# The first token half and two weight tiles of the second input projection, made ready inside the feed-forward's block

## The reference, cut to what matters

```
# end of the first block
h = rmsnorm(x, norm2_g)
u = h @ w_ffn_up
a, b = u[..., :D_FF], u[..., D_FF:]
a = causal_dwconv(a, ffn_conv_w, ffn_conv_b)
x = x + (silu(a) * b) @ w_ffn_down            # x2 in the kernel
x = rmsnorm(x, norm_f_g)                      # the first block's own last norm
# start of the second block
u = rmsnorm_2(x, norm1_g_2)
proj = u @ w_in_2                             # D_MODEL -> 37 tiles of 128 columns
x_r, y_r, c_q, c_kv, k_pe, g_a, g_b = split(proj)
x_r = causal_depthwise_conv(x_r, ...); h_r = rg_lru(x_r, ...)
```

## Time and profile before

| | us |
|---|---|
| median of 3 runs | 3498.38 |
| lowest and highest run | 3498.35, 3500.34 |
| the profiled execution, its time | 3503.13 |
| the profiled execution, its span | 3501.2 |
| TensorE busy in the span | 3125.2 (89%) |
| VectorE, ScalarE, GpSimd busy | 1609.1, 937.9, 440.9 |

### The profile page before, as it was taken

One profiled execution on the slowest core, in us unless ns is written; L12 is line 12 of the kernel. 1 busy time (PEld: TensorE's weight loads), 2 busy tenths in 40 slices (PEclk: granted clock), 3 DMA queues, 4 the chain that ended last, 5 costly groups with the idle time before them and its releaser, 6 DMA issues. The chain is left out here.

```text
span 3501.2 us, 47146 instructions
## 1 busy us (share of the span) xinstructions
PE 3125.2 (89%) x19758; PEld 2317.3 (66%) x19758; DVE 1609.1 (46%) x2278; ACT 937.9 (27%) x1349; POOL 440.9 (13%) x440
## 2 busy tenths in 40 slices
PE   7999779987999999997999997689979987878886
PEld 5778568876788888886778776466658863323232
DVE  6657335454566346634544445466543443111113
ACT  4333222223233222223333322133332211000000
POOL 2211002121000000002000001433201001111110
PEclk9999669998999999999999998799989997998997
DMA  3332331215333433334222234411046548999998
GB/s 124 115 127 97 122 93 29 74 33 183 108 97 98 140 123 97 97 118 141 79 82 75 79 114 154 165 61 61 31 144 208 181 151 320 423 423 424 424 391 342
DMA packets 147701, 555.41 MB, mean 159 GB/s; under 512 B 20544, under 2 KB 52992, under 8 KB 128424
## 3 DMA queue, kind: packets, MB, share of 16 engines
q1 hardware_dynamic: 105568, 426.79, 33.4%
q0 software_dynamic: 36800, 114.37, 8.7%
q10 hardware_dynamic: 5128, 11.30, 0.9%
HBM read 467.28 MB, written 105.02 MB: 163 GB/s over the span
## 5 line engine op out<-in xcount | busy, mean ns | idle before, releaser
L53 PE MATMUL in_acc<-in_x_hi,in_w_hi 128*128 128x512 f32 x1024 | 412.7, 403 | 40.4 <-DVE in_x_lo L1487 36.4
L55 PE MATMUL in_acc<-in_x_hi,in_w_lo 128*128 128x512 f32 x1024 | 403.3, 394 | 0.0
L54 PE MATMUL in_acc<-in_x_lo,in_w_hi 128*128 128x512 f32 x1024 | 403.3, 394 | 0.0
L1652 ACT CAST ff_w_hi<-ff_w_raw 128x1024 fp32r<-128x1024 f32 (+1 forms) x144 | 148.0, 1028 | 494.1 <-PE ff_acc L55 474.4
L53 PE MATMUL ff_acc<-ff_x_hi,ff_w_hi 128*128 128x512 f32 x704 | 275.3, 391 | 2.0 <-DVE ff_w_lo L1776 2.0
L54 PE MATMUL ff_acc<-ff_x_lo,ff_w_hi 128*128 128x512 f32 x704 | 274.6, 390 | 0.0
L55 PE MATMUL ff_acc<-ff_x_hi,ff_w_lo 128*128 128x512 f32 x704 | 274.4, 390 | 0.0
L53 PEld LDWEIGHTS in_acc<-in_x_hi,in_w_hi 128*128 128x128 f32 x1024 | 195.0, 190 | 92.3 <-issue 37.6
L1776 DVE TENSOR_TENSOR ff_w_lo<-ff_w_raw,ff_w_hi 128x1024 fp32r<-128x1024 f32 (+1 forms) x144 | 171.8, 1193 | 164.7 <-ACT ff_w_hi L1652 163.2
L54 PEld LDWEIGHTS in_acc<-in_x_lo,in_w_hi 128*128 128x128 f32 x1024 | 195.0, 190 | 44.7 <-issue 4.8
L55 PEld LDWEIGHTS in_acc<-in_x_hi,in_w_lo 128*128 128x128 f32 x1024 | 194.9, 190 | 41.4
(11 more groups left out here) (609 smaller groups left out, 5829.5 us busy)
## 6 DMA issues: line engine op xcount, KB each, us to landing
wide_b_lo<-in_w SPq DMA_DIRECT2D x24, 2048.0 KB, 40.0
wide_a_lo<-in_ew SPq DMA_DIRECT2D x48, 1024.0 KB, 37.8
wide_a_hi<-in_w SPq DMA_DIRECT2D x24, 2048.0 KB, 35.5
ff_w_raw<-in_w_up SPq DMA_DIRECT2D x88, 512.0 KB, 3.5
wide_b_hi<-in_w SPq DMA_DIRECT2D x20, 2048.0 KB, 36.7
in_w_raw<-in_w_in SPq DMA_DIRECT2D x64, 512.0 KB, 3.6
wide_w<-in_ew SPq DMA_DIRECT2D x20, 1024.0 KB, 38.5
ff_w_raw<-in_w_down SPq DMA_DIRECT2D x32, 512.0 KB, 3.6
```

Of the source, the lines that this page charges most:

```text
L53: pe.matmul(out, w_hi, x_hi, start=first, stop=False)
L54: pe.matmul(out, w_hi, x_lo, start=False, stop=False)
L55: return pe.matmul(out, w_lo, x_hi, start=False, stop=last)
L1652: nc.scalar.copy(w_hi[:, j % 3, 0:width], w_raw[:, j % 2, 0:width]).then_inc(w_hi_done, 1)
```

## The change

The second projection's preparations for the first 512 tokens move into the second half's down tiles of `feed_stage`, and what both stages use lies in tensors named `have_...` that outlive the feed-forward's block: `x_hi` and `x_lo` of 512 tokens, `w_raw`, `w_hi`, `w_lo`, both sums, the product of the gains and the squared inner gain.

In `feed_stage`, per down tile n of the second half: SyncE also loads the first half of tile n of x2; ScalarE makes `x_hi` and a square of it, and a square of the half tile that VectorE has just evicted (tile n - 1); VectorE makes `x_lo` and adds both squares into both sums. The units of weights are longer by two, the first two tiles of the second projection. GpSimd has nothing new.

In `in2` TensorE begins with the column matmuls, then makes the first two weight tiles over the first token half, spreads the factors, and then makes the same two tiles over the second token half. That half (`late_hi`, `late_lo`, from `late_raw`) is loaded and split in `in2` itself, behind the roots on ScalarE and behind the diagonals on VectorE. GpSimd's additions are gone.

```diff
-            load(0)
-            load(1)
-            for k in range(KT):
-                ...
-                sp.dma_start(x_raw[:, k % 4, :], src[k]).then_inc(x_loaded[k % 4], 16)
...
+                for k in range(KT):
+                    sp.dma_start(late_raw[:, k, :], src[k][:, HALF:]).then_inc(x_loaded[k], 16)
 # ScalarE of in2
+                for k in range(KT):
+                    act.wait_ge(x_loaded[k], 16)
+                    nc.scalar.activation(late_hi[:, k, :], late_raw[:, k, :], ACT.Copy, scale=gains[:, k:k + 1]).then_inc(x_hi_done, 1)
+                high_part(2)
             act.wait_ge(spread_ready, 1)
 # TensorE of in2
+                columns(0, sq_sum)
+                columns(DT, sum_2).then_inc(ss_ready, 1)
+                for k in range(KT):
+                    for j in range(2):
+                        mm = products(j, 0, k)
...
             mm.then_inc(spread_ready, 1)
+            if inner is not None:
+                for k in range(KT):
+                    pe.wait_ge(x_split, k + 1)
+                    for j in range(2):
+                        mm = products(j, 1, k)
...
             pe.wait_ge(rstd_ready, 2 if inner is not None else 1)
 # VectorE of in2
-                    dve.wait_ge(acc_ready, 2 * i + h + 1)
+                    dve.wait_ge(acc_ready, 2 * h + i + 1 if inner is not None and i < 2 else 2 * i + h + 1)
 # GpSimd of in2
-            for k in range(1, KT):
+            for k in range(1, KT if inner is None else 1):
 # feed_stage, weights
+    units += [(w, SEQ) for w in next_w]
 # SyncE of feed_stage
+            for k in range(DT):
+                sp.wait_ge(x_split, 2 * DT + k - 1)
+                if k >= 2:
+                    sp.wait_ge(half_sq_ready[0], k - 1)
+                sp.dma_start(x_raw[:, k % 2, :], x2[k][:, 0:HALF]).then_inc(x_loaded[k % 2], 16)
+                ...
+                        load(j)
 # ScalarE of feed_stage
+            def square_evicted(n):
+                act.wait_ge(acc_free, first_job["down", 1] + n + 1)
+                ...
+                nc.scalar.activation(half_sq[:, 1, n % 2, :], o_buf[:, n % 2, 0:HALF], ACT.Square).then_inc(half_sq_ready[1], 1)
...
+                    nc.scalar.activation(x_hi[:, n, :], x_raw[:, n % 2, :], ACT.Copy, scale=g).then_inc(x_hi_done, 1)
+                    if f == 1:
+                        ...
+                        nc.scalar.activation(half_sq[:, 0, n % 2, :], x_raw[:, n % 2, :], ACT.Square).then_inc(half_sq_ready[0], 1)
                     for c in range(CHUNKS):
                         high_part(j0 + CHUNKS * n + c + 3)
+                        if f == 1 and c == 0 and n >= 1:
+                            square_evicted(n - 1)
+            square_evicted(DT - 1)
 # VectorE of feed_stage
+            def add_half(h, n):
+                hs = slice(h * HALF, (h + 1) * HALF)
+                dve.wait_ge(half_sq_ready[h], n + 1)
+                ...
+                tt(sums[:, hs], sums[:, hs], half_sq[:, h, n % 2, :], ALU.add).then_inc(half_sum_ready[h], 1)
+                dve.wait_ge(half_sum_2_ready[h], n)
+                stt(out=sums_2[:, hs], in0=half_sq[:, h, n % 2, :], scalar=gain_sq[:, n:n + 1], in1=sums_2[:, hs], op0=ALU.mult,
+                    op1=ALU.add).then_inc(half_sum_2_ready[h], 1)
...
+                    if f == 1:
+                        add_half(0, n)
                     low_part(j0 + CHUNKS * n + 4)
+                    if f == 1 and n >= 1:
+                        add_half(1, n - 1)
...
+                    if f == 1 and n >= 2:
+                        dve.wait_ge(half_sq_ready[1], n - 1)
                     tt(o_buf[:, u, 0:HALF], acc[:, (q0 + n) % 4, :], aux[:, u, 0:HALF], ALU.add).then_inc(acc_free, 1)
+            add_half(1, DT - 1)
```

More of the change, by code:

```diff
@@ L1349, in norm_dense_stage @@
         aux = ctx.enter_context(nc.psum_tensor(f"{name}_aux", [P, 4, HALF], F32))
-        x_loaded = [sem(f"x_loaded{i}") for i in range(4)]
+        x_loaded = [sem(f"x_loaded{i}") for i in range(4 if inner is None else KT)]
         w_loaded = [sem(f"w_loaded{i}") for i in range(2)]
@@ new lines, in _ @@
+            if inner is None:
+                pe.wait_ge(w_lo_done, 2)
+                for k in range(KT):
+                    if k == KT - 1:
+                        pe.wait_ge(sum_ready, KT - 1)
+                        columns(0, sq_sum).then_inc(ss_ready, 1)
+                    pe.wait_ge(x_split, k + 1)
+                    for j in range(2):
+                        for h in range(NH):
+                            mm = products(j, h, k)
+                            if k == KT - 1:
+                                mm.then_inc(acc_ready, 1)
+            else:
+                columns(0, sq_sum)
+                columns(DT, sum_2).then_inc(ss_ready, 1)
+                for k in range(KT):
+                    for j in range(2):
+                        mm = products(j, 0, k)
@@ L1461, in _ @@
                 if i >= 2:
[L1462 removed]
+                    pe.wait_ge(w_lo_done, i + 1 - READY)
                     for h in range(NH):
@@ L1517, in _ @@
                                     ALU.mult).then_inc(diag_ready, 1)
+            if inner is not None:
+                for k in range(KT):
+                    dve.wait_ge(x_hi_done, k + 1)
+                    nc.vector.scalar_tensor_tensor(out=late_lo[:, k, :], in0=late_raw[:, k, :], scalar=gains[:, k:k + 1], in1=late_hi[:, k, :],
+                                                   op0=ALU.mult, op1=ALU.subtract).then_inc(x_split, 1)
+                low_part(2)
             side.vector_first(dve)
@@ L1639, in _ @@
                     load(j)
-            for j in range(first_unit["up", 1] + 3, NU):
+            for j in range(first_unit["up", 1] + 3, first_unit["down", 1] + 3):
                 load(j)
+            for u in range(2):
+                sp.wait_ge(stored[u], 16 * DT // 2)
+            for k in range(DT):
[3 more added lines that the diff above has]
+                sp.dma_start(x_raw[:, k % 2, :], x2[k][:, 0:HALF]).then_inc(x_loaded[k % 2], 16)
+                for c in range(CHUNKS):
+                    j = first_unit["down", 1] + 3 + CHUNKS * k + c
+                    if j < NU:
+                        load(j)
         @block.scalar
```

182 lines of the change are left out of this document (93 added, 89 removed).

## The result

Changed kernel: median 3488.12 us of 20 runs; kernel before, beside it: 3499.48 us of 20. The ratio is 0.9967, 95% interval 0.9959 to 0.9975: 0.33% or 11.4 us less, where 21.9 were forecast. The kernel is faster, as the likeliest sign was, but 3488.1 lies outside the range that ended at 3482.0.

A forecast was written before the change was run, and what follows sets the result against it. TensorE was taken to bound the second projection from tile i = 2 on; starting that tile 20.2 us earlier, plus 1.65 us of half clock, gave 21.9 us: 3498.4 less 21.9 is 3476.5 us, range 3470.5 to 3482.

The forecast's parts named there:

- The feed-forward's block at no cost: Feed-forward's down tiles: the added VectorE, ScalarE and load work fits into idle time, so the block ends as before.
- (a): From the feed-forward's last matmul (1620.8) to the second projection's first column matmul (1625.5): 4.7 us, as now.
- B: Rival, less gained: the feed-forward's block ends late (store's issue held) or half clock lasts longer; 3479 to 3481 us, chance 0.17.
- (b): Second projection's 32 one-column matmuls, 5 at full clock and 27 at half: 6.3 us.
- (c): Second projection's 48 matmuls over the first token half, 4.4 us of them at half clock: 13.0 us.
- (d): Second projection's two spreads of the factors, between the matmuls of both token halves: 3.5 us.
- (e): Second projection's 48 matmuls over the second token half, at 0.227 us each: 10.9 us.
- Behind i = 2 the half clock: Second projection, behind the start of tile i = 2: the half clock goes, as no wait stands ahead; 1.65 us gained.
- The gate's slack: Recurrent layer's gate behind tile i = 2: work of 10.0 us ahead of it against the tile's 10.9 leaves 0.9 us.
- A: Rival, faster: the second projection's column matmuls keep the clock up, 4.9 us less, 3471.6 us; chance 0.15.
- C: Rival, hardly a change: convolution's chain sets the pace, recurrent work gives time back; some 3492 to 3500 us, chance 0.04.
- D: Rival, slower: added VectorE work makes TensorE wait in each of the 8 down tiles; 3505 us, chance 0.03.

The follow-up runs named there:

- a_pad192: The changed kernel with 192 unused bytes per partition behind the shared tensors, and nothing else: 3478.6 us, ratio 0.9942.
- gains_first: The changed kernel with the two 32-byte tensors (gains, gain_sq) allocated ahead of the shared operands instead of behind them: 3481.8 us, ratio 0.9949.
- a_pad192_b: A repetition of a_pad192 with the same code: 3480.2 us, ratio 0.9942.
- warm_cols: a_pad192 with five unused 128x512 float32 matmuls behind the feed-forward's last product, in TensorE's idle time ahead of the columns: ratio 0.9932.
- a_pad32: The changed kernel with 32 unused bytes behind the shared tensors: 3495.8 us, ratio 0.9986.

## Why the prediction was right or wrong

**What bounds the kernel: right.** The seam and the projection stood on TensorE, and an earlier i = 2 was passed on.

**The feed-forward's block at no cost: right for the work, wrong for the block.** With the distance at zero and the added work in place, the feed-forward takes 814.5 us from its first to its last matmul in `a_pad192`, 814.9 in `gains_first` and 815.4 in `a_pad192_b`, against 814.4 before; the four kernels with other columns or unused matmuls have 812.6 to 815.2. So five operations on VectorE, three on ScalarE and the loads of each down tile cost nothing that could be told from the scatter of 1 us. But the changed kernel took 818.6: 3.2 us from the pace and about 1 from a longer half clock at the start. The sign "the last eviction of the feed-forward at the same time as now, to 0.5 us" failed: 1624.47 against 1621.10. Two of the prediction's own signs of a wrong sum came true as well: the evictions in the down tiles drift, by 0.15 us a tile, and the first column starts at 1628.96, past 1626.5.

**(a)** 4.7 us forecast, 4.9 measured (1624.10 to 1628.96). The last store was issued at 1625.45, 0.3 us behind the last eviction. B's held issue didn't come, but it wasn't put to the test either: only the issue's last 0.14 us lie beside an addition, which starts at 1625.85.

```profile
1625.45 0.54 POOL L1976 DMA_DIRECT2D s_x<-ff_o_buf  x1 [14.57 <-DVE ff_o_buf L1947]
```

**(b)** 6.3 forecast, 6.8 measured: all 32 columns at half clock, 0.213 us each. The fall lay ahead of the first one. Two columns in 0.44 us, the row of the attention, are 0.22 each, where the sum used 0.21.

**(c)** 13.0 forecast, 13.3 measured, with 4.8 us at half clock where I took 4.4.

**(d)** 3.5 forecast; 3.0 until the first large matmul behind them, which takes 0.4 us more than a later one.

**(e)** 10.9 forecast, 11.4 measured (1652.11 to 1663.50): this 0.4, and 48 matmuls of 229.6 ns instead of 226.7.

Together 39.4 us instead of 38.4. Behind i = 2 the half clock did go. The eviction of that tile comes 14.5 us behind its start, where it was 15.6: 1.1 us, where 1.65 were forecast. So the seam's own terms were 1.6 us too kind.

**The gate's slack: right.** Its matmuls start at 1674.48 us without idle time.

**The step that failed** is the pace of the large matmuls. The sum has 0.227 us for each in (c) and (e), and gives the down tiles and the tiles behind i = 2 no term at all: their pace was taken to stay as it was. The change moves f, the late half and the weights to other addresses. I counted what operations were added and what waited, and took the cadence of the rows of before as a property of the engine. It was a property of the layout too: 228.9 ns in the down tiles and 229.1 on the mean in the second projection, instead of 226.7. 3.2 us in the feed-forward and 4.2 in the second projection (the 48 of (e) among them) went there, 7.4 in all; by the ratios of the padded kernels it is 6 to 9. The sum then reads: 21.9 forecast, less 7.4 for the pace, less 1.6 for the seam, is 12.9 us (0.1 of (e) is counted in both); the profiles show 12.3, the medians 11.4.

**The rivals.** A is out: `warm_cols` gave the columns a full clock and they lost it. The prediction weighed the Trainium skill, "TensorE: Matmul & The Clock Gate", "What's actually happening", by which activity releases the throttle. By that rule read plainly `warm_cols` would have won 5.2 us; it won 3.3, and the large matmuls behind 3.57 us of nothing but columns ran at half clock for 3.4 us. Here 32 such columns didn't keep the clock up, and in the changed kernel 6.8 us of them didn't bring it back. B's time was nearer, but not by its mechanisms: the block didn't end late for a store, and the half clock added 0.8 us in (b) and (c). C and D: no wait of TensorE shows either; in `a_pad32`, with 32 unused bytes, C's time would have come true by the pace alone.

With the pace restored, `gains_first` measures 17.9 us less (an interval of 12 to 24) and `a_pad192` 20.3 (15 to 26). The forecast of 21.9 lies in both.

## What to carry to other kernels

In this kernel a matmul's cadence belonged to the layout as well as to the engine: when a change moves a streamed or a stationary operand, compare their addresses modulo 256 before and after, and allocate small tensors where they don't come between the large ones. When a gain is missing and no wait is to be found, divide the time between two evictions by the matmuls between them, in both kernels; a difference of 1% per matmul is invisible in a row of 0.39 us and plain in a tile. One-column matmuls neither held nor earned the clock here, so the price of a stretch of columns takes in a half clock of some 3 to 5 us behind it.
